# Two low-rank products side by side: decay and rate products of both directions paired on TensorE in a bidirectional recurrence

## The chip, the cores and the metric

The kernel runs on one core of one Trainium2 chip. The metric is the time of one execution on the device in microseconds (us), the median of the runs shown. PE is TensorE (its weight loads are listed apart as PEld), DVE VectorE, ACT ScalarE, POOL GpSimd and SP SyncE.

## What is computed

The program is one inference step of a two-layer backbone over 384 tokens: 128 context tokens and 256 latent tokens, with the same weights. Each layer is a SwiGLU feed-forward block, three token mixers from one input projection (grouped attention, differential attention, a bidirectional RWKV-7 recurrence), their gated merge, and a second feed-forward block. The change is inside the recurrence. Cut to what matters there:

```
w_logit = w0[d] + tanh(wl[:, d]) @ w2[d]           # decay, a low-rank product (rank 64) for each direction d
decay   = exp(-exp(-softplus(-w_logit) - 0.5))
a       = sigmoid(a0[d] + al[:, d] @ a2[d])        # rate, a low-rank product (rank 64) for each direction d
# for each head and direction, over time:
sa = S @ (-kk_t)
S  = S * w_t + outer(sa, kk_t * a_t) + outer(v_t, k_t)
o_t = S @ r_t
```

The product before the decay is 384 tokens by rank 64 by 512 channels, for two directions; the one before the rate is of the same size.

## The kernel before

The 512 channels of the recurrence are worked in four blocks (j = 0 to 3, NB = 4) of 128 channels, two heads of 64 each. In each layer one loop over j holds everything. The 384 tokens are cut into NQ = 6 chunks of 64. In block j the kernel builds the chunk products (`gram`, six parts p = 0 to 5, three of each direction), inverts the triangular systems of all chunks in five doubling levels (`level_lx`, `level_xlx`), and turns keys for later use (`turn_tok`). Between these pieces it runs the scan over chunks of the block before, s = j - 1 (`scan_right`, `scan_solve`, `scan_update`, four steps each, i = 0 to 3), and prepares decay, rate and norm of the block after, j + 1 (`prepare_decay`, `prepare_rate`, `prepare_norm`). Block 0 has no scan beside it, block 3 has no preparation in it, and the scan of block 3 runs alone behind the loop.

The order on each engine is the order in which the code is written, and engines meet only through semaphores. The same loop is written out once for PE, once for ACT, once for DVE and once for POOL. For one direction d of the block to come, PE makes the decay product (`prepare_decay`, L1221), ACT takes its tanh out of the bank into `sg` (L1723), POOL scales it (L2012), and DVE sums it over time (L2400) and centres the sums (L2405 to L2412). The rate product (L1229) goes through a tanh of ACT into `aa` (L1732), and then, behind the second level, through `key_factor` on ACT, POOL and DVE.

The quarter-size matmuls of the recurrence are issued by `quads` (L1166): one on partitions 0 to 63 and one on partitions 64 to 127. Each float32 matmul of the program stands in the trace as two MATMUL instructions. The two low-rank weights of decay lie in `lora_w`, direction 0 on partitions 0 to 63 and direction 1 on partitions 64 to 127, and so do their inputs, and the same holds for `lora_a`; so a decay or rate product reads 64 partitions and writes all 128 of a bank of 384 columns.

The eight banks of PSUM are `acc[0..3]` and `pb[0..3]`. In blocks 1 to 3 both directions of the decay share `acc[3]`, one after the other, so that PE waits for ACT's read between them. The rates use `acc[1]` (direction 0) and `acc[0]` (direction 1). `gram` part p uses `pb[(p + 2) % 4]`. For block 0 the two decay products stand one behind the other, into `pb[2]` and `pb[3]`, ahead of the loop, and so do its two rate products.

## Time and profile before

| | us |
|---|---|
| median of three runs (lowest, highest) | 2705.01 (2704.34, 2706.89) |
| the profiled execution, its own time | 2699.4 |
| its span, from first to last instruction | 2695.2 |
| loop over the blocks, layer 1 | 753.3 to 951.5 |
| scan of the last block, layer 1 | 951.5 to 967.5 |
| start of the loop, layer 2 | 2078.1 |

PE is busy for 94% of the span, DVE for 52%, ACT for 39%, POOL for 12%; the mean granted clock of TensorE is 0.965 of full speed. A busy share is an average over all stages. Times within the span are read from the timeline; a matmul's end is modelled, so distances on PE are best taken from start to start.

### The profile page before, as it was taken

Reading aid. Unit: us, or ns where it says so; the run is one execution under the profiler, and the core shown is the slowest. Engines: PE = TensorE matmul, PEld = TensorE weight load, DVE = VectorE, ACT = ScalarE, POOL = GpSimd, SP = SyncE. Lnnn points to the kernel's source line nnn. Section 1 sums busy time; section 2 is a strip of 40 time slices with the busy share of each in tenths; the row PEclk is TensorE's granted clock in tenths of the full one; section 3 lists DMA queues with packets and bytes.
Section 4 is the critical chain, followed back from the end, with each engine's and each line's share of the span. In section 5 each row is a group of like instructions: output and inputs, shape, how many; then the busy total and the mean of one; then the engine's idle time right before and its main releaser. Section 6 shows DMA issues by size and latency. Waiting matters only on the chain. (4 is left out here: it accounts for less than half of the span.)

```text
span 2695.2 us, 56725 instructions
## 1 busy us (share of the span) xinstructions
PE 2524.0 (94%) x23398; PEld 2350.4 (87%) x23398; DVE 1389.2 (52%) x2314; ACT 1056.5 (39%) x1705; POOL 332.1 (12%) x316
## 2 busy tenths in 40 slices
PE   5999999999979989999979999999998999899998
PEld 3889989889968878999968899998897888889997
DVE  3334365576576645443353334656765775544434
ACT  3333244355533424332253333434564342343323
POOL 0000032000033304000100001210001341130001
PEclk7999999999989988999989999999998999889998
DMA  8766634233200013446466665333221001234373
GB/s 270 244 219 194 189 96 125 85 89 87 88 2 4 27 45 93 126 126 202 121 211 220 225 189 156 98 108 96 83 84 62 4 4 30 80 100 127 116 218 106
DMA packets 482186, 319.95 MB, mean 119 GB/s; under 512 B 15474, under 2 KB 438920, under 8 KB 481800
## 3 DMA queue, kind: packets, MB, share of 16 engines
q1 hardware_dynamic: 481928, 316.32, 38.7%
q8 instruction: 186, 3.05, 0.5%
q14 instruction: 72, 0.59, 0.1%
HBM read 311.30 MB, written 4.98 MB: 117 GB/s over the span
## 5 line engine op out<-in xcount | busy, mean ns | idle before, releaser
L826 PE MATMUL acc<-xm_hi,w_hi 128*128 128x384 f32 x2512 | 866.8, 345 | 54.1 <-DVE xm_lo L2086 33.1
L828 PE MATMUL acc<-xm_hi,w_lo 128*128 128x384 f32 x2512 | 850.0, 338 | 0.0
L827 PE MATMUL acc<-xm_lo,w_hi 128*128 128x384 f32 x2448 | 826.7, 338 | 0.0
L2076 DVE TENSOR_TENSOR w_lo<-raw,w_hi 128x1024 fp32r<-128x1024 f32 (+1 forms) x420 | 519.7, 1237 | 503.7 <-ACT w_hi L1524 495.4
L826 PEld LDWEIGHTS acc<-xm_hi,w_hi 128*128 128x128 f32 x2512 | 479.3, 191 | 97.4 <-issue 59.0
L1524 ACT ACTIVATE w_hi<-raw 128x1024 fp32r<-128x1024 f32 (+1 forms) x420 | 439.6, 1047 | 301.6 <-PE acc L828 220.2
L828 PEld LDWEIGHTS acc<-xm_hi,w_lo 128*128 128x128 f32 x2512 | 478.8, 191 | 0.0
L827 PEld LDWEIGHTS acc<-xm_lo,w_hi 128*128 128x128 f32 x2448 | 466.6, 191 | 0.5
L826 PE MATMUL acc<-h_hi,w_hi 128*128 128x384 f32 x704 | 242.5, 345 | 8.6 <-DVE w_lo L2076 8.6
L827 PE MATMUL acc<-h_lo,w_hi 128*128 128x384 f32 x704 | 239.7, 341 | 0.0
L828 PE MATMUL acc<-h_hi,w_lo 128*128 128x384 f32 x704 | 239.7, 340 | 0.0
L1555 ACT ACTIVATE sa<-acc 128x384 f32<-128x384 f32 x88 | 43.3, 492 | 448.4 <-PE acc L828 448.2
L826 PEld LDWEIGHTS acc<-h_hi,w_hi 128*128 128x128 f32 x704 | 133.8, 190 | 19.8 <-issue 18.6
L827 PEld LDWEIGHTS acc<-h_lo,w_hi 128*128 128x128 f32 x704 | 134.0, 190 | 0.0
L828 PEld LDWEIGHTS acc<-h_hi,w_lo 128*128 128x128 f32 x704 | 133.7, 190 | 0.0
L2163 DVE TENSOR_TENSOR hf<-sa,acc 128x384 f32<-128x384 f32 x88 | 48.8, 554 | 160.6 <-PE acc L828 155.4
L1962 POOL TENSOR_TENSOR ln_sum<-x 128x384 f32<-128x384 f32 x12 | 17.2, 1431 | 920.7 <-DVE x L2099 920.5
L2008 POOL TENSOR_TENSOR ltm<-lt,cst 128x384 f32<-128x384 f32 x80 | 87.4, 1092 | 169.4 <-PE pb L1166 97.0
L2099 DVE SCALAR_TENSOR_TENSOR x<-acc,modv,x 128x128 f32<-128x128 f32 x96 | 35.7, 413 | 127.8 <-PE acc L828 127.4
L2012 POOL TENSOR_SCALAR sg<-sg 128x384 f32<-128x384 f32 x16 | 9.1, 568 | 609.8 <-ACT sg L1723 609.6
L1782 ACT ACTIVATE tl<-pb 128x384 f32<-128x384 f32 x80 | 39.3, 492 | 102.8 <-PE pb L1166 102.7
L1166 PE MATMUL pb<-xi,ltm 64*64 64x64 f32 x1920 | 71.5, 220 | 5.6 <-DVE xt L2471 2.8
(340 smaller groups left out, 3268.1 us busy)
## 6 DMA issues: line engine op xcount, KB each, us to landing
raw<-in_ffn_w_in SPq DMA_DIRECT2D x179, 512.0 KB, 4.0
modw<-in_w_mod SPq DMA_DIRECT2D x71, 1024.0 KB, 6.2
raw<-in_w_in SPq DMA_DIRECT2D x114, 512.0 KB, 4.1
raw<-in_ffn_w_out SPq DMA_DIRECT2D x64, 512.0 KB, 4.9
raw<-in_ffn_w_out SPq DMA_DIRECT2D x32, 384.0 KB, 3.5
raw<-in_w_up SPq DMA_DIRECT2D x24, 512.0 KB, 3.5
modx<-in_w_mod SPq DMA_DIRECT2D x9, 1024.0 KB, 12.8
raw<-in_w_out SPq DMA_DIRECT2D x16, 512.0 KB, 4.1
```

Source lines behind the costliest of these rows:

```text
L826: pe.matmul(out, lhs[0], rhs[0], start=first, stop=False)
L827: pe.matmul(out, lhs[0], rhs[1], start=False, stop=False)
L828: return pe.matmul(out, lhs[1], rhs[0], start=False, stop=last)
L1166: mm = pe.matmul(out[hp], lhs[hp], rhs[hp], start=start, stop=stop, skip_group_check=True)
L1524: done(act.activation(w_hi[:, c % SPL, 0:w], raw[:, c % RAW, 0:w], ACT.Copy), hi_done)
L1555: freed(act.activation(sa[:, j % 2, :], gbank(ka)[:, 0:TOK], ACT.Silu), ka)
L1782: done(act.activation(tl[:, NQ * d:NQ * d + NQ, :].rearrange("p q s -> p (q s)"), pb[d][:, 0:TOK], ACT.Copy), tl_ready)
L1962: add = lambda out, a, b: pool.tensor_tensor(out, a, b, ALU.add)
L2008: done(pool.tensor_tensor(ltm[:, u, :], lt[:, u, :], over(cst[:, o:o + CH], NQ), ALU.mult), ltm_ready)
L2076: done(dve.tensor_tensor(w_lo[:, c % SPL, 0:w], raw[:, c % RAW, 0:w], w_hi[:, c % SPL, 0:w].bitcast(F32), ALU.subtract), lo_done)
L2099: ins = dve.scalar_tensor_tensor(out=x[:, m, a:b], in0=gbank(key)[:, a:b], scalar=modv[:, 3 * s + 2, m, gi:gi + 1], in1=x[:, m, a:b], op0= ...
L2163: freed(dve.tensor_tensor(hf[:, j % 2, :], sa[:, j % 2, :], gbank(kb)[:, 0:TOK], ALU.mult), kb)
```

## The change

The decay product of direction 1 moves up, to stand right behind that of direction 0, and gets a bank of its own, `pb[1]`. The rate product of direction 0 moves down, to stand right ahead of that of direction 1; their banks, `acc[1]` and `acc[0]`, stay. ACT's tanh of the rate of direction 0 moves with it; ACT's two decay tanhs keep their places and read the new bank. Waits follow: the second decay product no longer waits for ACT's read of the first, but for the last reader of `pb[1]` in the block before (`xt_ready`, for block 0 `kk_ready`); `gram` part 3, which is next to write `pb[1]`, waits for both tanhs (`decay_done`), and `turn_tok`, the next to write `acc[3]`, for the first only. No instruction is added or taken out.

```diff
@@ -1213,9 +1213,11 @@
                         if j == 0:
                             bank = pb[2 + d]
                         else:
-                            bank = acc[3]
-                            if d == 1:
-                                pe.wait_ge(decay_done, 2 * j + 1)
+                            bank = (acc[3], pb[1])[d]
+                            if d == 1 and j == 1:
+                                pe.wait_ge(kk_ready, 1)
+                            elif d == 1:
+                                pe.wait_ge(xt_ready, 2 * (NL + 1) * (j - 1))
                             elif j >= 3:
                                 pe.wait_ge(out_done, j - 2)
@@ -1236,8 +1238,10 @@
                             pe.wait_ge(ab_ready, 2 * j + d + 1)
                         if p >= 4:
                             pe.wait_ge(gram_read, n - 3)
+                        elif p == 3 and j + 1 < NB:
+                            pe.wait_ge(decay_done, 2 * j + 4)
                         elif j == 0:
-                            pe.wait_ge((rate_done, rate_done, kk_std, kk_ready)[p], (1, 2, 1, 1)[p])
+                            pe.wait_ge((rate_done, rate_done, kk_std)[p], (1, 2, 1)[p])
@@ -1256,7 +1260,7 @@
                         if k >= 1:
                             pe.wait_ge(tok_ready, 4 * j + k)
                         elif j + 1 < NB:
-                            pe.wait_ge(decay_done, 2 * j + 4)
+                            pe.wait_ge(decay_done, 2 * j + 3)
@@ -1412,11 +1416,10 @@
                         if nxt:
                             prepare_decay(j + 1, 0)
+                            prepare_decay(j + 1, 1)
                         gram(j, 1)
                         if old:
                             scan_solve(s, 0)
-                        if nxt:
-                            prepare_decay(j + 1, 1)
                         gram(j, 2)
@@ -1443,8 +1446,6 @@
                         if old:
                             scan_right(s, 3)
-                        if nxt:
-                            prepare_rate(j + 1, 0)
                         level_lx(j, 1, 1)
@@ -1454,6 +1455,7 @@
                             scan_update(s, 3)
                         if nxt:
+                            prepare_rate(j + 1, 0)
                             prepare_rate(j + 1, 1)
                         level_xlx(j, 1, 1)
@@ -1719,7 +1721,7 @@
-                        bank = acc[3] if j >= 1 else pb[2 + d]
+                        bank = (acc[3], pb[1])[d] if j >= 1 else pb[2 + d]
@@ -1860,8 +1862,6 @@
                         if old:
                             scan_right(s, 3)
-                        if nxt:
-                            prepare_rate(g0)
                         level_lx(j, 1, 1)
                         copy_tok(j, 1, 1)
@@ -1870,6 +1870,7 @@
                         if old:
                             copy_new(s)
                         if nxt:
+                            prepare_rate(g0)
                             prepare_rate(g1)
```

The decay pair on PE, in block 1. Line numbers of the kernel before and of the changed one differ by two from there on. Before, from the end of the first `scan_right` on (`lora_w` is the decay product, `ar,bt` and `ar,kt` are `gram` parts, `rs,xt` is `scan_solve`):

```order
L1166 MATMUL acc<-ar,sp 64x64 x4
L1221 MATMUL acc<-cmix,lora_w 128x384
L1166 MATMUL pb<-ar,bt 64x128 [waits xi_ready]
L1166 MATMUL pb<-ar,bt 64x128
L1166 MATMUL pb<-ar,kt 64x128 x2
L1166 MATMUL pb<-ar,bt 64x128 x2
L1166 MATMUL pb<-ar,kt 64x128 x2
L1166 MATMUL acc<-rs,xt 64x64 [waits xt_ready,r_ready]
L1166 MATMUL acc<-rs,xt 64x64 x7
L1221 MATMUL acc<-cmix,lora_w 128x384 [waits decay_done]
L1166 MATMUL pb<-ar,bt 64x128 [waits xt_ready]
L1166 MATMUL pb<-ar,bt 64x128
```

After:

```order
L1166 MATMUL acc<-ar,sp 64x64 x4
L1223 MATMUL acc<-cmix,lora_w 128x384
L1223 MATMUL pb<-cmix,lora_w 128x384 [waits xt_ready]
L1166 MATMUL pb<-ar,bt 64x128 [waits xi_ready]
L1166 MATMUL pb<-ar,bt 64x128
L1166 MATMUL pb<-ar,kt 64x128 x2
L1166 MATMUL pb<-ar,bt 64x128 x2
L1166 MATMUL pb<-ar,kt 64x128 x2
L1166 MATMUL acc<-rs,xt 64x64 [waits xt_ready,r_ready]
L1166 MATMUL acc<-rs,xt 64x64 x7
L1166 MATMUL pb<-ar,bt 64x128 [waits xt_ready]
L1166 MATMUL pb<-ar,bt 64x128
```

The second decay product now stands ahead of `gram` part 1 and of `scan_solve`, in `pb`.

The rate pair on PE, in block 0. Before (`xi,ltm` is `level_lx`, `cst,kt` is `turn_tok`, `tl,xt` and `xt,tl` are `level_xlx`, `lora_a` is the rate product):

```order
L1166 MATMUL pb<-xi,ltm 64x64 [waits xi_ready,ltm_ready]
L1166 MATMUL pb<-xi,ltm 64x64 x11
L1229 MATMUL acc<-cmix,lora_a 128x384
L1166 MATMUL pb<-xi,ltm 64x64 [waits xi_ready,ltm_ready]
L1166 MATMUL pb<-xi,ltm 64x64 x11
L1166 MATMUL acc<-cst,kt 64x64 [waits tok_ready]
L1166 MATMUL acc<-cst,kt 64x64 x11
L1166 MATMUL pb<-tl,xt 64x64 [waits gram_read,xt_ready,tl_ready]
L1166 MATMUL pb<-tl,xt 64x64 x11
L1166 MATMUL pb<-xt,tl 64x64 x12
L1229 MATMUL acc<-cmix,lora_a 128x384
```

After:

```order
L1166 MATMUL pb<-xi,ltm 64x64 [waits xi_ready,ltm_ready]
L1166 MATMUL pb<-xi,ltm 64x64 x11
L1166 MATMUL pb<-xi,ltm 64x64 [waits xi_ready,ltm_ready]
L1166 MATMUL pb<-xi,ltm 64x64 x11
L1166 MATMUL acc<-cst,kt 64x64 [waits tok_ready]
L1166 MATMUL acc<-cst,kt 64x64 x11
L1166 MATMUL pb<-tl,xt 64x64 [waits gram_read,xt_ready,tl_ready]
L1166 MATMUL pb<-tl,xt 64x64 x11
L1166 MATMUL pb<-xt,tl 64x64 x12
L1231 MATMUL acc<-cmix,lora_a 128x384 x2
L1166 MATMUL pb<-tl,xt 64x64 [waits gram_read,xt_ready,tl_ready]
```

The first rate product has left its place between the two halves of `level_lx` and stands beside the second.

ACT's side of the rates, in block 1. Before (`tl` is the copy behind `level_lx`, `aa` the tanh of a rate, `cs` and `sg` exponentials of the decay, `osum` the copy of the scan's output):

```order
L1782 ACTIVATE tl<-pb 128x384 [waits tl_done,tok_ready]
L1788 ACTIVATE rs<-acc 128x128 [waits r_done,tl_ready]
L1732 ACTIVATE aa<-acc,half_bias 128x384 [waits ab_ready,lora_rate,r_ready]
L1782 ACTIVATE tl<-pb 128x384 [waits tl_done,rate_done]
L1777 ACTIVATE ktok<-acc 128x384 [waits tok_t,tl_ready]
L1752 ACTIVATE cs<-zi 128x384 [waits z_ready,tok_ready]
L1757 ACTIVATE sg<-sg 128x384 [waits act_chain]
L1799 ACTIVATE sld<-acc 128x2x64 [waits spo_t,act_chain]
L1732 ACTIVATE aa<-acc,half_bias 128x384 [waits ab_ready,lora_rate,snew_ready]
L1795 ACTIVATE osum<-acc 128x384 [waits o_done,rate_done]
L1782 ACTIVATE tl<-pb 128x384 [waits tl_done,o_read]
L1782 ACTIVATE tl<-pb 128x384 [waits tl_done,tl_ready]
```

After:

```order
L1784 ACTIVATE tl<-pb 128x384 [waits tl_done,tok_ready]
L1790 ACTIVATE rs<-acc 128x128 [waits r_done,tl_ready]
L1784 ACTIVATE tl<-pb 128x384 [waits tl_done,r_ready]
L1779 ACTIVATE ktok<-acc 128x384 [waits tok_t,tl_ready]
L1754 ACTIVATE cs<-zi 128x384 [waits z_ready,tok_ready]
L1759 ACTIVATE sg<-sg 128x384 [waits act_chain]
L1801 ACTIVATE sld<-acc 128x2x64 [waits spo_t,act_chain]
L1734 ACTIVATE aa<-acc,half_bias 128x384 [waits ab_ready,lora_rate,snew_ready]
L1734 ACTIVATE aa<-acc,half_bias 128x384 [waits ab_ready,lora_rate,rate_done]
L1797 ACTIVATE osum<-acc 128x384 [waits o_done,rate_done]
L1784 ACTIVATE tl<-pb 128x384 [waits tl_done,o_read]
L1784 ACTIVATE tl<-pb 128x384 [waits tl_done,tl_ready]
```

The tanh of direction 0 now comes behind the exponentials and the copy of the state, right ahead of that of direction 1 and of the copy of `osum`.

## Rows read from the trace of the kernel before

**Rows 1.** The page of the profile: head, and the engines of the chain that ended last.

```profile
span 2695.2 us, 56725 instructions
...
PE 42%; DVE 4%; ACT 1%; SPq 1%; issue 1%; DMA 0%; POOL 0%; DVEq 0%; ACTq 0%; POOLq 0%
```

**Rows 2.** Busy time by stretch: length, PE, PEld, DVE, ACT, POOL, PEclk, DMA share, GB/s.

```profile
753.20:764.20 11.00, 10.90 (x92) 7.99 (x92) 5.49 (x9) 2.49 (x6) 2.72 (x4) 0.54 0.01 1
...
796.79:849.10 52.31, 50.73 (x1335) 45.58 (x1334) 35.82 (x66) 22.02 (x45) 17.06 (x18) 1.00 0.01 4
```

**Rows 3.** Timeline of PE ahead of block 0: start, duration, what, [idle before].

```profile
734.95 0.92 PE L1221 MATMUL pb<-cmix,lora_w 64*128 64x384 f32 x4
735.79 0.44 PE L826 MATMUL acc<-br_hi,w_hi 128*128 128x384 f32 x1
```

**Rows 4.** Timeline of PE, block 1 (801 to 805) and block 2 (863 to 865).

```profile
801.85 0.63 PE L1166 MATMUL acc<-rs,xt 64*64 64x64 f32 x16
802.41 0.91 PE L1221 MATMUL acc<-cmix,lora_w 64*128 64x384 f32 x2
803.25 0.43 PE L1166 MATMUL pb<-ar,bt 64*64 64x128 f32 x4
803.52 0.39 PE L1166 MATMUL pb<-ar,kt 64*64 64x128 f32 x4
...
804.17 0.63 PE L1166 MATMUL acc<-sas,btok 64*64 64x64 f32 x16
...
863.50 0.63 PE L1166 MATMUL acc<-rs,xt 64*64 64x64 f32 x16
863.97 0.39 PE L1166 MATMUL pb<-ar,bt 64*64 64x128 f32 x4
864.19 0.39 PE L1166 MATMUL pb<-ar,kt 64*64 64x128 f32 x4
```

**Rows 5.** Timeline of DVE, blocks 0 and 1, and the last recurrence.

```profile
771.02 0.56 DVE L2458 TENSOR_TENSOR xi<-pb,cst 128x384 f32<-128x384 f32 x1
...
803.09 0.42 DVE L2492 COPY sas<-acc 128x256 f32<-128x256 f32 x1
...
816.64 0.29 DVE L2492 COPY sas<-acc 128x128 f32<-128x128 f32 x1 [0.28 <-PE acc L1166]
...
955.43 0.42 DVE L2492 COPY sas<-acc 128x256 f32<-128x256 f32 x1 [1.89 <-PE acc L1166]
```

**Rows 6.** Timeline of PE, last recurrence of layer 1.

```profile
955.91 0.68 PE L1166 MATMUL acc<-sas,btok 64*64 64x64 f32 x16 [0.59 <-DVE sas L2492]
```

**Rows 7.** Timeline of PE, start of block 0 of layer 1.

```profile
758.67 1.64 PE L1221 MATMUL acc<-cmix,lora_w 64*128 64x384 f32 x2
760.24 0.69 PE L1166 MATMUL pb<-ar,bt 64*64 64x128 f32 x4
...
762.00 1.44 PE L1166 MATMUL acc<-cst,bt 64*64 64x64 f32 x24
763.28 0.38 PE L1166 MATMUL pb<-ar,bt 64*64 64x128 f32 x4
```

**Rows 8.** Timeline of PE around rate products, blocks 0 and 1.

```profile
771.28 0.91 PE L1229 MATMUL acc<-cmix,lora_a 64*128 64x384 f32 x2
772.12 0.92 PE L1166 MATMUL pb<-xi,ltm 64*64 64x64 f32 x24
...
819.88 0.45 PE L1166 MATMUL acc<-sp,ar 64*64 64x64 f32 x8 [1.06 <-DVE sp L2475]
...
820.73 0.91 PE L1229 MATMUL acc<-cmix,lora_a 64*128 64x384 f32 x2
821.57 0.91 PE L1166 MATMUL pb<-xi,ltm 64*64 64x64 f32 x24
```

**Rows 9.** Timeline of ACT behind the second rate product, block 1.

```profile
826.82 0.49 ACT L1795 ACTIVATE osum<-acc 128x384 f32<-128x384 f32 x1
828.48 0.49 ACT L1782 ACTIVATE tl<-pb 128x384 f32<-128x384 f32 x1 [1.16 <-PE pb L1166]
```

## The prediction

> **What bounds the kernel now.** I read the page first, then the busy times by stretch, then the timelines of PE, DVE, ACT and POOL through the recurrence. The span is 2695.2 us, and in the chain that ended last PE has 42% of the span against 4% for DVE; no DMA share is seen in it [rows 1]. For this change only the loop over the blocks counts, so the next view is the busy time by stretch. In block 1 PE is busy for 50.73 of 52.31 us, at a granted clock of 1.00, with a DMA share of 0.01 [rows 2]. DVE has 35.82 us there, ACT 22.02, POOL 17.06. So PE sets the pace nearly all the time, and what is taken off PE comes off the time, as long as DVE and ACT, which must answer it, do not come too late at some place. Those places have to be looked for one by one in the timelines. The reader is to see there where PE's next instruction starts, and where the result it needs is ready.
>
> **What one low-rank product costs, and what a pair costs.** A product alone, of direction 1 in block 1, starts at 802.41 and the next instruction at 803.25: 0.84 us [rows 4]. Ahead of block 0 the trace holds the very pair that the change makes: four MATMULs, both directions, into two banks. They start at 734.95 and what follows starts at 735.79: again 0.84 us [rows 3]. Two products behind each other cost what one costs, since they read different halves of the partitions. So in each pair one product is free.
>
> The change saves a little more than 0.84, since each product also has borders with the quarter-size matmuls around it. From the start of a solve (L1166, 16 MATMULs) to the second group of `gram` matmuls it is 801.85 to 803.52, 1.67 us, with a product between; without one, in block 2, the same two pieces take 863.50 to 864.19, 0.69 us [rows 4]. The difference is 0.98 us: that is what PE itself saves when a product leaves its place. The page "TensorEngine Tiling (Array Packing)" of the Trainium skill, section Key Properties, says that a change of tiling mode drains TensorE. The 0.14 us by which 0.98 exceeds 0.84 agrees with it; by the page's "up to 2x" of the section Theoretical Speedup alone one would count 0.84 for a pair, 10.1 us for twelve.
>
> There are three preparations in a layer (blocks 0, 1 and 2), two kinds, two layers: 12 pairs. I follow each to the next place where PE waits.
>
> **Decays in blocks 1 and 2.** The pair takes the place of the first product, so `gram` part 1 and `scan_solve` start when they did. Behind the solve `gram` part 2 starts 0.98 earlier, and so could `scan_update`, now at 804.17 [rows 4], at 803.19. But it needs the solved states that DVE copies (L2492): that copy runs from 803.09 to 803.51 [rows 5], and it does not get earlier, because what it waits for (`gram` part 1 and the solve) stands ahead of the removed product. From the end of such a copy to PE's start it is 0.06 us: 955.43 + 0.42 = 955.85, and 955.91 [rows 5, 6]. So the update starts at 803.57 and the gain here is 0.60 instead of 0.98; PE gets a new wait of 0.38 behind this copy. Block 2 repeats the pattern. Four times 0.60 is 2.4 us.
>
> Does the 0.60 last? Behind this point DVE is at times the late one: PE waits 1.06 us at 819.88 for the new state [rows 8]. But DVE's run of work that ends in that state starts with the copy at 816.64, which itself waited for PE [rows 5]. So the wait moves forward with PE and stays 1.06.
>
> The added waits: the second decay product asks for the last level of the block before, which DVE wrote before PE came to the first product; `gram` part 3 asks for both tanhs of ACT, and two pieces of PE work stand between. I cost both at nothing. Late, each would hold all of PE behind it, one for one; I keep up to 0.3 us each for four places, 1.2 us, as the bad bound.
>
> **Decays in block 0.** There is no scan beside it, and nothing behind the removed product waits for its neighbours. But TensorE has just stood still, waiting for DVE, and runs at the low level: the granted clock is 0.54 over the first 11 us, which is 1.2 GHz for nearly all of it and 2.4 GHz only from about 763 on [rows 2]. The product takes 1.57 us there, 758.67 to 760.24; a later piece that starts at 762.00 takes 1.28, and from 763.28 on all is short [rows 7]. If the rise comes at the same moment of the stage as before, the slow stretch is as long as before, and what moves into it in place of the product would have been run at the full clock later: then the gain is that of the full clock, 0.98, say 1.0. If the rise came after the same amount of work instead, the gain would be 1.57 and borders, about 1.7. I take 1.0, since the rows show the clock rising in the middle of a piece of work and at no border of it. Twice, 2.0 us, with 3.4 as the upper end. Further on in block 0 PE waits for DVE, but that run of DVE's work starts from ACT's copy of `gram` part 3, which moves with PE.
>
> **Rates in blocks 1 and 2.** The product at 820.73 goes, and `level_lx` of direction 1 starts in its place [rows 8]. What it reads has been ready: its `xi` is written right before the state for which PE waited at 819.88 [rows 8]. Behind it come a turn of keys, the solve, and the first half of a level, whose inputs from ACT are copies that move up too. So the whole 0.98 stays, four times: 3.9 us.
>
> What the moved tanh can do on ACT: at its new place ACT has two tanhs, then the copy of `osum`, which ended at 827.31, then the copy behind level 2, which started at 828.48 after 1.16 us of waiting for PE [rows 9]. One tanh more, about 0.6 us (two of these copies' 0.49 or a little more), fits into 1.16. So I cost it at nothing; without that cover, up to 0.1 us per block.
>
> **Rates in block 0.** Here the cover is thinner. `level_lx` of direction 1 starts at 772.12 behind the product at 771.28 [rows 8]; it could start 0.98 earlier, but its `xi` is written by DVE from 771.02 to 771.58 [rows 5], and 0.06 later is 771.64. Its gain is 0.48. DVE's run of work ahead of it moves with PE. Twice, 1.0 us.
>
> **The sum.** 2.4 + 2.0 + 3.9 + 1.0 = 9.3 us, from 12 pairs that would give 11.8 at 0.98 each if nothing were late. The stages behind the recurrence start from its last output through DVE, ACT and POOL, so they move as a whole, and their weights are asked for as PE frees buffers. Against the profiled execution (span 2695.2, own time 2699.4) that is 2685.9 and 2690.1. The median of the runs shown is 5.6 above that execution's own time, and I keep this distance: 2705.0 - 9.3 = 2695.7 us.
>
> **The rivals.**
> A, the forecast, 2695.7; its own range is 2693.0 to 2698.5. Chance 0.68.
> B, nothing is late and the slow stretch gives back fully: 8 x 0.98 + 2 x 0.98 + 2 x 1.7 = 13.2 us, 2691.8. For it: DVE has 16 us of free time in a block. Against it: the two copies of [rows 5] stand at fixed places. Chance 0.08.
> C, a shift is lost on the way. If the DVE or ACT runs do not move with PE (their backlog starts earlier than I read), the decays' 2.4 and half of the rest go: about 5 us remain, 2700. For it: the 1.06 us wait shows that DVE is late at one place in each of these blocks. Against it: DVE waited for PE at 816.64 [rows 5]. Chance 0.14.
> D, the change does not do what it says: `acc[3]` with `pb[1]`, or the wait between the two products, keeps them apart, and a pair takes 2 x 0.84. Then a product is only moved. The rates give nothing; the decay pair delays `gram` part 1, the solve and DVE's copy by 0.84, the update is then late by about 0.4 in four places, and the time is 2705 + 1.6 = 2706.6. Against it: the pair of [rows 3], and the same for rates ahead of block 0. Chance 0.05.
> E, slower: the clock. In block 0 PE's first 10 us run at 1.2 GHz; with two products side by side its work there has another mix. If the slow stretch lasted twice as long, work of 5 us at the full clock would cost 10, 5 us more per layer, and 10 us in all would outweigh the 9.3: 2705.7; it decides from about 9 us of further slow time in each layer. Later stages rise from 1.2 GHz too, and each could come out a microsecond or two away from before, to either side; that together with this could bring 2708. Against it: a removed product leaves no gap, PE goes on without a pause (10.90 of 11.00 us busy, [rows 2]). The page "TensorE: Matmul & The Clock Gate" of the Trainium skill, in its Part 1, says that the clock follows how busy the engine has been; no row here shows that a pair counts as less busy. Chance 0.05.
>
> **How the numbers follow.** Range: A and the part of C and B next to it, 2691.5 to 2700.5, leaves out half of B, D, E and the far part of C, about 0.18. About 0.2% (5.4 us) is what a measurement of this kernel tells from no change. Faster by more than that: A, B and a third of C, 0.81. Within it: the rest of C, D and part of E, 0.16. Slower: 0.03.
>
> **What would show it.** In the changed kernel's timeline of PE: groups of four MATMULs of 64x384 that last 0.84 from start to start (1.57 in block 0's decays), six per layer in the loop; a wait of about 0.4 for DVE's copy L2492 (two lines further on) ahead of the first `scan_update` in blocks 1 and 2; a short wait ahead of the second `level_lx` of block 0; the 1.06 wait for the state unchanged. Block 1 should last 52.31 - 1.6 = 50.7 us from first `gram` to first `gram`, block 2 1.6 less, block 0 1.5 less, block 3 the same. The prediction is wrong if block 3 or the stages behind change, if a pair lasts 1.6 at the full clock, or if the wait for the state grows by what was saved before it.

## The result, and the profile after

The changed kernel takes 2689.51 us (median of four runs, 2685.39 to 2691.22); the kernel before, run beside it, takes 2704.68 (2703.26 to 2706.89). The ratio over the single runs is 0.9941, with a 95% interval of 0.9926 to 0.9957, so the change is a gain of about 0.6%: 15.2 us in this first comparison, where 9.3 were predicted. The time lies below the predicted range of 2691.5 to 2700.5. More runs of both, further down, make the difference 13.2.

Page of the changed kernel, the lines that answer to [rows 1], and the busy time of the engines:

```profile
span 2686.4 us, 56725 instructions
...
PE 2513.9 (94%) x23398; PEld 2347.4 (87%) x23398; DVE 1392.8 (52%) x2314; ACT 1054.1 (39%) x1705; POOL 328.4 (12%) x316
...
PE 42%; DVE 4%; ACT 1%; SPq 1%; issue 1%; DMA 0%; POOL 0%; DVEq 0%; ACTq 0%; POOLq 0%
```

The number of instructions and the shape of the chain have not changed. The next view is the busy time by stretch, as in [rows 2]: the first 11 us of block 0 in layer 1, then the same in layer 2.

```profile
754.40:765.40 11.00, 10.05 (x172) 8.56 (x174) 8.28 (x14) 3.53 (x9) 2.71 (x4) 0.85 0.01 1
...
2076.00:2087.00 11.00, 10.46 (x153) 8.86 (x155) 7.08 (x12) 3.04 (x8) 2.63 (x4) 0.72 0.01 1
```

PE does 172 instructions there in place of 92, at a granted clock of 0.85 in place of 0.54. No instruction was taken out, so this is the first sign that the gain is not only that of products side by side: PE also comes to the full clock earlier. The timeline of PE shows where the clock rises, in layer 1:

```profile
754.49 0.69 PE L1166 MATMUL pb<-ar,bt 64*64 64x128 f32 x4 [12.18 <-DVE kt L2437]
...
756.39 1.00 PE L1223 MATMUL acc<-cmix,lora_w 64*128 64x384 f32 x1
756.40 1.00 PE L1223 MATMUL pb<-cmix,lora_w 64*128 64x384 f32 x1
...
757.86 0.44 PE L1166 MATMUL pb<-ar,bt 64*64 64x128 f32 x4
758.13 0.39 PE L1166 MATMUL pb<-ar,kt 64*64 64x128 f32 x4
...
769.68 0.92 PE L1166 MATMUL pb<-xi,ltm 64*64 64x64 f32 x24 [0.37 <-DVE xi L2459]
```

The first `gram` group lasts 0.69, which is the low level (1.2 GHz); right behind the decay pair, 3.37 us after the block's start, the same group lasts 0.44, which is the high one (2.4 GHz). Before, `gram` groups were still long at 760.24, 6.9 us after the start, and short only at 763.28, 10.0 us after it [rows 7]. In layer 2 the rise comes 6.08 us after the start, at 2082.10. The last row is the short wait for `xi` ahead of the second `level_lx`.

Block 1 at full clock, where the steps of the prediction can be read singly:

```profile
797.47 0.59 PE L1223 MATMUL acc<-cmix,lora_w 64*128 64x384 f32 x1
797.48 0.59 PE L1223 MATMUL pb<-cmix,lora_w 64*128 64x384 f32 x1
...
798.32 0.44 PE L1166 MATMUL pb<-ar,bt 64*64 64x128 f32 x4
...
800.36 0.39 PE L1166 MATMUL pb<-ar,kt 64*64 64x128 f32 x4
800.96 0.68 PE L1166 MATMUL acc<-sas,btok 64*64 64x64 f32 x16 [0.22 <-DVE sas L2493]
...
816.74 0.45 PE L1166 MATMUL acc<-sp,ar 64*64 64x64 f32 x8 [1.08 <-DVE sp L2476]
...
821.08 0.92 PE L1231 MATMUL acc<-cmix,lora_a 64*128 64x384 f32 x4
821.93 0.92 PE L1166 MATMUL pb<-tl,xt 64*64 64x64 f32 x24
```

And DVE at the place that bounds the update:

```profile
800.48 0.42 DVE L2493 COPY sas<-acc 128x256 f32<-128x256 f32 x1
```

Both products of a direction pair start within 0.01 us of each other, and what follows starts 0.85 after the first (797.47 to 798.32, and again 821.08 to 821.93). The copy ends at 800.90 and the update starts at 800.96.

The lengths of the blocks carry the rest. In this table a block goes from its first `gram` to the first `gram` of the next, and "rise" is the time from the start of block 0 to the first group of matmuls that is short. The whole recurrence goes from the start of block 0 to the start of the last group of matmuls in the last scan.

| layer 1 / layer 2, us | rise | block 0 | block 1 | block 2 | block 3 | whole recurrence |
|---|---|---|---|---|---|---|
| before (second profile) | 9.8 / 9.8 | 43.49 / 43.49 | 52.88 / 52.88 | 53.32 / 53.31 | 48.35 / 48.36 | 213.54 / 213.52 |
| after (second profile) | 3.4 / 6.1 | 39.87 / 40.89 | 51.36 / 51.36 | 51.79 / 51.81 | 48.37 / 48.37 | 206.87 / 207.91 |

The recurrence (the four blocks and the last scan) gives 6.67 + 5.61 = 12.3 us. Block 3 and the last scan (15.5 us) are as before.

### The profile page after: what moved, and what is told of

It is laid out like the page before. It is cut to its first block and busy times, and to the rows that moved or that the text cites. A ratio compares the mean times of both kernels' runs of the same rounds, so it can differ in the third digit from the quotient of the medians.

```text
span 2686.4 us, 56725 instructions
## 1 busy us (share of the span) xinstructions
PE 2513.9 (94%) x23398; PEld 2347.4 (87%) x23398; DVE 1392.8 (52%) x2314; ACT 1054.1 (39%) x1705; POOL 328.4 (12%) x316
```

## The experiments

Times are medians, each with the kernel before beside it on the same chip; n is the number of runs. The ratio, with its 95% interval in brackets, is formed over the single runs and can differ a little from that of the two medians. Lengths of blocks and rises come from the one profiled execution of each kernel. Spare products read the same inputs as real ones. The result of every spare product or matmul is overwritten unread, so the outputs do not change.

**1. Both kernels again, unedited.**

> The kernel before, unchanged, profiled and timed again, to see how much one profiled execution differs from the next. Theory 1 (the paired product makes TensorE's clock rise earlier in block 0): block 0 of both layers again lasts about 43.5 us from first gram to first gram, with the granted clock rising some 9 to 10 us after its start, and the time is 2704 to 2705. Theory 2 (the moment of the rise varies from execution to execution, whatever the kernel): block 0's slow stretch differs from the 9 to 10 us seen by a few us in at least one layer, and single executions scatter by several us.

> The changed kernel, unchanged, profiled and timed again. Theory 1: block 0 again rises to the full clock 3 to 6 us after its start and lasts about 40 to 41 us, against 43.5; the median is about 2690, 14 to 15 us below the kernel before. Theory 2: the slow stretch of block 0 falls anywhere between 3 and 10 us; over more executions the gain settles nearer to 9 to 10 us (2695), which is what the pairs save at the full clock.

Before again: 2703.41 (n 11) against 2702.70 (n 23), ratio 0.9999 [0.999, 1.0008], so the comparison itself is even. After again: 2689.48 (n 5) against 2702.70, 0.9946 [0.9932, 0.9959], 13.2 us. The spans of these two profiles, 2699.5 and 2686.7, differ by 12.8, of which the table gives 12.3 to the recurrence. Single executions scatter: those of the kernel before lie between 2697.34 and 2704.55 here. The profile on which the prediction's sum rests (span 2695.2) was one 4.3 us below this one, with the same lengths inside the recurrence to 0.2 us; it spent less time at the low clock elsewhere (mean granted clock 0.965 against 0.960). So the comparison of four runs with four holds scatter, and the recurrence is what the change moves.

**2. The change without its decay pair in block 0.** From the changed kernel; in block 0 the second product keeps its old place and bank (the waits of `gram` part 3 and `turn_tok` and ACT's bank follow, not shown).

```diff
-                            bank = (acc[3], pb[1])[d]
+                            bank = (acc[3], pb[1] if j >= 2 else acc[3])[d]
                             if d == 1 and j == 1:
-                                pe.wait_ge(kk_ready, 1)
+                                pe.wait_ge(decay_done, 3)
...
-                            prepare_decay(j + 1, 1)
+                            if old:
+                                prepare_decay(j + 1, 1)
                         gram(j, 1)
                         if old:
                             scan_solve(s, 0)
+                        else:
+                            prepare_decay(j + 1, 1)
```

> The change, but in block 0 the two decay products stay apart as before (into one bank). Theory 1: block 0 goes back to a slow stretch of 9 to 10 us and the time rises by 2 x 3 = 5 to 6 us over the changed kernel, to about 2695. Theory 2: only the product's own saving of about 1 us per layer is lost, 2 us over the changed kernel, and the slow stretch scatters as in the others.

2694.18 (n 7) against 2702.70, 0.9972 [0.9961, 0.9983]; span 2689.1. Timeline of PE in block 0:

```profile
757.01 1.64 PE L1223 MATMUL acc<-cmix,lora_w 64*128 64x384 f32 x2
...
760.48 1.64 PE L1223 MATMUL acc<-cmix,lora_w 64*128 64x384 f32 x2
...
763.82 1.13 PE L1166 MATMUL acc<-cst,bt 64*64 64x64 f32 x24
764.78 0.38 PE L1166 MATMUL pb<-ar,bt 64*64 64x128 f32 x4
```

The rise is back at 9.7 / 9.8 us and block 0 at 43.12 / 43.10, while blocks 1 and 2 keep their gain. The pair in block 0 alone is thus worth 43.12 - 39.86 = 3.26 and 43.10 - 40.86 = 2.24, together 5.5 us, where I had put 2.0. What is left in block 0, 43.49 - 43.11, is the rate pair's 0.38.

**3. Only the pair of block 0.** From the kernel before (ACT's bank follows).

```diff
-                            bank = acc[3]
-                            if d == 1:
+                            bank = pb[1] if j == 1 and d == 1 else acc[3]
+                            if d == 1 and j == 1:
+                                pe.wait_ge(kk_ready, 1)
+                            elif d == 1:
...
                             prepare_decay(j + 1, 0)
+                            if j == 0:
+                                prepare_decay(j + 1, 1)
...
-                        if nxt:
+                        if nxt and old:
                             prepare_decay(j + 1, 1)
```

> The kernel before with the decay pair in block 0 alone. Theory 1: gains 2.2 to 3.2 us per layer, about 5.5 us in all, 2699, with the clock rising 3 to 6 us after the start of block 0. Theory 2: gains about 1 us per layer, 2 us in all, 2703.

2697.94 (n 11) against 2702.70, 0.9981 [0.9972, 0.999]: 4.8 us. Block 0 lasts 40.26 / 41.27, the rise is at 3.4 / 6.1, and blocks 1 and 2 are as before. In the recurrence that is 3.2 + 2.2 = 5.4 us.

**4. Only the rate pairs.** From the kernel before, both `prepare_rate` as in the change (ACT's too).

```diff
-                        if nxt:
-                            prepare_rate(j + 1, 0)
                         level_lx(j, 1, 1)
...
                         if nxt:
+                            prepare_rate(j + 1, 0)
                             prepare_rate(j + 1, 1)
```

> The kernel before with the rate pairs alone, decays as before. By the prediction's steps block 0 is shorter by 0.4 to 0.5 us and blocks 1 and 2 by 0.98 us each: 43.1, 51.9 and 52.3 us. A rival, that the moved tanh on ACT or the later rate costs something further on: less than that, with a wait of PE for ACT behind the second level.

This kernel was executed once, in 2691.55 us. Single executions scatter too much for that to tell a gain; the lengths of the blocks do tell. Blocks 1 and 2 last 51.89 and 52.34, so 0.99 and 0.98 less than before, in both layers; block 0 lasts 43.11 / 43.12, 0.38 less. Rates in all: 4 x 0.98 + 2 x 0.38 = 4.7 us (predicted 4.9). What the decays add in the full change is then 51.89 - 51.36 = 0.53 in block 1 and 52.34 - 51.80 = 0.54 in block 2.

**5. Is it the saved work, or what stands beside it?** Two kernels from the one before, with a spare product in block 0 behind the first: on the other half of the partitions, so that it runs beside the real one, or on the same half, so that it runs behind it. Nothing is saved in either.

```diff
                             prepare_decay(j + 1, 0)
+                            if j == 0:
+                                pe.wait_ge(kk_ready, 1)
+                                pe.matmul(pb[1][:, 0:TOK], lora_w[HALVES[1], 128:256], cmix[HALVES[1], 12, :], start=True, stop=True)
```

(`HALVES[0]` in both places for the product behind.)

> The kernel before, with one spare decay product of direction 1 (its result is overwritten unread) issued right behind the first decay product of block 0 into the free bank pb[1]; both real products stay where they were. Theory 1a (two products side by side bring the clock's rise forward): nothing is saved in work, yet block 0 rises to the full clock 3.4 us (layer 1) and 6.1 us (layer 2) after its start, and lasts about 41.2 and 42.2 us against 43.5, 3 to 4 us less in all. Theory 1b (it is the missing second product, so a change of what follows, that matters): the rise stays at 9.8 us and block 0 at 43.5.

> The same, but the spare product reads the same half of the partitions as the first one (direction 0 again), so that the two can't run side by side and take 3.1 us at the low clock instead of 1.6. Theory 1a: no two halves are at work at once, so the rise stays at 9 to 10 us after the start, and block 0 is 0.8 to 1.6 us longer than 43.5. A third reading (any more work early on brings the rise forward): the rise comes early here too.

Timeline of PE with the spare product beside:

```profile
756.43 1.00 PE L1221 MATMUL acc<-cmix,lora_w 64*128 64x384 f32 x1
756.44 1.00 PE L1417 MATMUL pb<-cmix,lora_w 64*128 64x384 f32 x1
...
757.89 0.44 PE L1166 MATMUL pb<-ar,bt 64*64 64x128 f32 x4
...
758.91 0.91 PE L1221 MATMUL acc<-cmix,lora_w 64*128 64x384 f32 x2
```

The same in layer 2, where all of the pair runs at the low clock:

```profile
2077.90 1.00 PE L1221 MATMUL acc<-cmix,lora_w 64*128 64x384 f32 x1
2077.91 1.00 PE L1417 MATMUL pb<-cmix,lora_w 64*128 64x384 f32 x1
...
2079.48 0.69 PE L1166 MATMUL pb<-ar,bt 64*64 64x128 f32 x4
```

And with the spare product behind, in layer 1:

```profile
756.90 1.64 PE L1221 MATMUL acc<-cmix,lora_w 64*128 64x384 f32 x2
758.34 1.48 PE L1417 MATMUL pb<-cmix,lora_w 64*128 64x384 f32 x2
```

Beside, block 0 falls from 43.49 to 40.89 / 42.21 with the rise at 3.4 / 6.5, although all the old work and one product more are still there. In layer 2 the second real product, which stands alone, starts 5.4 us after the block's start and is running when the clock rises. Behind, block 0 grows to 45.59 / 45.36 with the rise at 13.8 / 13.6. The pair takes 2077.90 to 2079.48, 1.58 us, as long as the lone product of the kernel before (1.57 us, [rows 7]) and in its place, so it is not the length of the lone product that holds the rise back, but the missing neighbour.

The run with the spare product beside also splits the 3.23 and 2.22 us that block 0 won in experiment 3: 2.60 and 1.28 come from the clock alone, and 40.89 - 40.26 = 0.63 and 42.21 - 41.27 = 0.94 from the product that is gone. The medians are 2702.21 (n 10), 0.9997 [0.9988, 1.0006], and 2707.47 (n 10), 1.0013 [1.0004, 1.0022], against 2703.60. The second agrees with its blocks (about +4). The first gains less than its two recurrences do (210.93 + 212.61 against 427.06, 3.5 us): its profiled execution was the fastest of the ten, and whether the rise comes as early in the other nine stays open. By the medians alone, this kernel is not told from the kernel before.

**6. Does it take a pair at all?** Three orders of block 0's start. First, from the changed kernel, the pair behind `gram` part 1 and the solve:

```diff
-                            prepare_decay(j + 1, 0)
-                            prepare_decay(j + 1, 1)
                         gram(j, 1)
                         if old:
                             scan_solve(s, 0)
+                        if nxt:
+                            prepare_decay(j + 1, 0)
+                            prepare_decay(j + 1, 1)
```

(ACT takes the two tanhs behind its `gram` copy as well.)

> The changed kernel with the decay pair moved behind gram part 1 and scan_solve (on PE) and both tanhs behind the copy of gram part 1 (on ACT). If the step on DVE's copy was right (that copy bounded the gain to 0.6 in blocks 1 and 2, because its inputs stood ahead of the product), the wait of 0.22 ahead of the first scan_update goes, and blocks 1 and 2 are about 0.4 us shorter each, and block 2 by up to 0.4 more since the product no longer waits for osum; 1.6 to 2.4 us in all. If the copy was not the bound, blocks 1 and 2 stay at 51.4 and 51.8. In block 0 the pair comes about 1.9 us later, which by theory 1a may put off the clock's rise by one to three us.

```profile
757.07 0.45 PE L1166 MATMUL pb<-ar,kt 64*64 64x128 f32 x4
757.45 0.59 PE L1223 MATMUL acc<-cmix,lora_w 64*128 64x384 f32 x1
...
849.88 0.68 PE L1166 MATMUL acc<-rs,xt 64*64 64x64 f32 x16 [0.89 <-ACT rs L1790]
```

The clock rises at 3.0 / 6.1, in layer 1 before the pair comes: `gram` parts 0 and 1 on end are enough. 2689.07 (n 5) against 2703.60, 0.9942 [0.9928, 0.9955], which the scatter does not tell from the changed kernel's time. Block 1 is 0.43 shorter than in the changed kernel, since DVE's copy is now hidden behind the pair. Block 2 gains nothing and is 0.17 longer, as the last row shows: the solve stands too early for ACT's copy `rs` and waits 0.89. So the 1.6 to 2.4 us that were expected did not come.

Second, therefore, the pair between `gram` part 1 and the solve:

```diff
                         gram(j, 1)
+                        if nxt:
+                            prepare_decay(j + 1, 0)
+                            prepare_decay(j + 1, 1)
                         if old:
                             scan_solve(s, 0)
```

> The changed kernel with the decay pair between gram part 1 and scan_solve (on PE), both tanhs behind the copy of gram part 1 (on ACT). In the run before, the pair behind the solve took away the wait for DVE's copy but gave block 2 a wait of 0.9 us for ACT's copy ahead of the solve. Here the pair covers that one as well, and gram part 2 (0.87 us) covers the way from the solve over DVE's copy to the update (0.28 + 0.42 + 0.06 = 0.76 us). If the waits are what bounds: block 1 about 50.9 us, block 2 about 50.95 us (against 51.36 and 51.8), 1.2 us less per layer, block 0 as in the run before (40.0 and 40.9), the median about 2 us below the changed kernel. If something else bounds them, blocks 1 and 2 stay above 51.3.

Both waits are gone, and so is one of 0.4 us for DVE's `osum` ahead of block 2's first product, which both kernels of the comparison have: block 1 lasts 50.93, block 2 51.07, against 51.36 and 51.80 of the changed kernel. The recurrence is 205.63 / 206.74. Timed, 2690.10 (n 5) against 2703.23, 0.9956 [0.9942, 0.9969]: the 2.4 us by which its recurrence beats the changed kernel's do not stand out of the scatter, and the median about 2 us below the changed kernel's did not show.

Third, from the kernel before, no pair anywhere: in block 0 PE does `gram` part 0, part 1, then a lone product, part 2, the other lone product (ACT in the same order).

```diff
-                        if nxt:
+                        if nxt and old:
                             prepare_decay(j + 1, 0)
...
                         if nxt:
-                            prepare_decay(j + 1, 1)
+                            prepare_decay(j + 1, int(old))
                         gram(j, 2)
+                        if not old:
+                            prepare_decay(1, 1)
```

> The kernel before, with block 0's two decay products moved later and kept apart: gram parts 0 and 1, product, gram part 2, product, turn_tok. No pair anywhere in the loop. Theory 1a (side by side work brings the rise forward) expects the rise at 9 to 10 us after the start, as in the kernel before, and block 0 at 43.5. Theory 1b' (it is a lone product, which keeps only half of the rows at work for 1.6 us at the low clock, that holds the rise back, and gram parts alone do not) expects layer 1 to rise at about 3.0 us, as when gram parts 0 and 1 followed each other, and block 0 of layer 1 at about 40.9 (two lone products at the full clock); layer 2 rose later than layer 1 in every kernel with a pair, and may rise at 6 or at 9 us.

```profile
756.25 0.69 PE L1166 MATMUL pb<-ar,bt 64*64 64x128 f32 x4 [12.18 <-DVE kt L2440]
...
759.26 0.67 PE L1166 MATMUL pb<-ar,kt 64*64 64x128 f32 x4
759.86 0.91 PE L1221 MATMUL acc<-cmix,lora_w 64*128 64x384 f32 x2
...
763.35 0.92 PE L1166 MATMUL acc<-cst,bt 64*64 64x64 f32 x24 [0.72 <-ACT sg L1725]
```

The rise is at 3.6 in layer 1 and under 3 in layer 2 (6 or 9 were expected there), the first lone product is already short, and block 0 lasts 41.16 / 40.81, in spite of a new wait of 0.72 for ACT. 2694.92 (n 6) against 2703.23, 0.9969 [0.9957, 0.9981]. So the pair is not what brings the rise forward. What is common to all early cases is that no product stands alone in the first 5 us of the slow stretch.

**7. The counter-test.** From `pair_before_solve`'s order, with its pair, one lone spare product ahead of `gram` part 1.

```diff
+                        if j == 0:
+                            pe.matmul(acc[3][:, 0:TOK], lora_w[HALVES[0], 128:256], cmix[HALVES[0], 12, :], start=True, stop=True)
                         gram(j, 1)
```

> The version with the pair between gram part 1 and the solve, in which block 0 rose to the full clock at 2.6 to 3.0 us (layer 1) and 6.1 us (layer 2), plus one spare lone decay product of direction 0 in block 0 between gram part 0 and gram part 1 (overwritten unread). Theory 1b' (a lone product early in the stretch holds the rise back): the rise goes back to 9 to 10 us in both layers and block 0 to about 43 to 44 us, though the pair is still there behind gram part 1. Theory 1a (a pair brings it forward, or any early work does): the rise stays at or below 6 to 7 us and block 0 at 41.5 to 42.5 us, longer only by the spare product's own 1.6 us at the low clock.

```profile
758.07 1.64 PE L1418 MATMUL acc<-cmix,lora_w 64*128 64x384 f32 x2
...
761.55 1.00 PE L1223 MATMUL acc<-cmix,lora_w 64*128 64x384 f32 x1
...
763.12 0.69 PE L1166 MATMUL pb<-ar,bt 64*64 64x128 f32 x4
...
764.88 1.22 PE L1166 MATMUL acc<-cst,bt 64*64 64x64 f32 x24
765.94 0.38 PE L1166 MATMUL pb<-ar,bt 64*64 64x128 f32 x4
```

One product alone puts the rise back to 9.8 / 9.8, with the pair in place, and block 0 to 43.11 / 43.09: 3.31 and 2.17 us more than without it, for 1.6 us of work. 2692.61 (n 9) against 2703.40, 0.9954 [0.9941, 0.9968]; the medians of the two kernels, 10.8 and 13.1 us below the kernel before, differ in the same direction.

**8. No slow stretch.** Block 0 starts slow because PE has waited 12.2 us for DVE. From the changed kernel, that wait is filled with 15 spare matmuls on all 128 partitions; then the same 15, and 18, in the order of `pair_before_solve`.

```diff
+                pe.wait_ge(kk_std, 1)
+                for _ in range(15):
+                    pe.matmul(pb[0][:, 0:TOK], blk, cmix[:, 12, :], start=True, stop=True)
```

> The changed kernel with 15 spare full-size matmuls (overwritten unread) in PE's wait of 12.2 us ahead of block 0. If the slow stretch comes from PE standing still there, block 0 runs at the full clock from its start, and is shorter by half of the slow 3.4 and 6.1 us: about 1.6 and 2.9 us, 4.5 us in all, 2685. If not, it stays at 39.9 and 40.9 us.

> The same with the 15 spare matmuls in the wait ahead of block 0, the best version that the runs point to. Blocks 38.3, 50.9, 50.95, 48.4 and 15.5 us in both layers, 204.1 against 206.9 and 207.9 of the changed kernel, 6.5 us less in all; median about 2683 to 2685.

> The version with the pair between gram part 1 and the solve and 18 instead of 15 spare full-size matmuls in the wait ahead of block 0: the 15 took 9.94 us and left 2.3 us of standing still, in which the clock fell in one layer of one execution and not in the other three. 18 take 11.9 us of the 12.2. Expected: block 0 at the full clock from its start in both layers, 38.3 to 38.5 us, the whole recurrence 204.2 us per layer, median 2683 to 2685. If the fall has nothing to do with the gap, one of the layers starts slow again.

With 15, `spare_in_wait` runs block 0 at full clock from its start, 38.35 / 38.36 us; 2686.97 (n 5) against 2703.60, 0.9945 [0.9931, 0.9959]. The same 15 in `pair_before_solve_warm` do it in layer 2 only (38.49); in layer 1, busy time by stretch from the last spare on:

```profile
751.00:754.36 3.36, 1.01 (x5) 0.29 (x3) 3.26 (x4) 0.00 (x0) 3.11 (x4) 0.97 0.00 0
754.36:758.00 3.64, 3.64 (x34) 3.47 (x36) 3.36 (x6) 0.33 (x2) 0.56 (x1) 0.56 0.02 5
```

The 15 leave 2.35 us of waiting, and behind it the clock is 0.56 (the last column but two); block 0 takes 40.02. The other three waits of 2.3 us, in the other layer and in `spare_in_wait`, were followed by the full clock. 2687.00 (n 5) against 2703.23, 0.9942 [0.9928, 0.9955]. With 18 the wait left is 0.39:

```profile
742.41 11.88 PE L1411 MATMUL pb<-cmix,cst 128*128 128x384 f32 x36
754.68 0.44 PE L1166 MATMUL pb<-ar,bt 64*64 64x128 f32 x4 [0.39 <-DVE kt L2439]
```

Both layers start at full clock (38.49 / 38.48). The recurrence is 205.41 / 204.32 (block 3 of layer 1 has a 0.8 us gap for which the profile shows no releaser), and the kernel takes 2684.17 us (n 6, 2678.42 to 2685.20) against 2703.40, ratio 0.9925 [0.9909, 0.994]. It has the lowest median of this study: 19.2 us below the kernel before beside it, where the changed kernel was 13.2 below its own. Of the 6.0 between them the recurrences account for 206.87 + 207.91 - 205.41 - 204.32 = 5.1. The intervals of the two ratios still touch (0.9909 to 0.994 and 0.9932 to 0.9959), so the lengths of the blocks, more than the medians, show that it is faster.

## Why the prediction was right, and where it failed

**A pair costs what one product costs.** Right: 0.85 for 0.84. Rival D, where a pair would take twice as long, is out.

**Decays in blocks 1 and 2.** Predicted 0.60 each, bounded by DVE's copy; measured 0.53 and 0.54 in each layer, 2.1 us in all for 2.4. The update itself starts 7.21 us after block 1's start before (second profile) and 6.61 after, so the 0.60 is there; the last 0.06 goes right behind the wait, where the update's own group takes 0.52 to the next start in place of 0.46. The new wait ahead of the update is there (listed as 0.22, since ends of matmuls are modelled; the groups before step by 0.22, so my estimate of the end of the last is 800.58, and of the wait 0.38). Experiment 6 shows the mechanism from the other side: with the pair behind `gram` part 1, so that it covers the copy, block 1 wins 0.43 more.

**Rates in blocks 1 and 2.** Predicted 0.98 each, measured 0.98 to 0.99. **Rates in block 0.** Predicted 0.48, measured 0.38. The wait for `xi` is there, 0.37; DVE ends it at 769.53 and PE starts at 769.68, 0.15 behind it, where I had taken 0.06:

```profile
768.97 0.56 DVE L2459 TENSOR_TENSOR xi<-pb,cst 128x384 f32<-128x384 f32 x1
```

**What was costed at nothing.** Right. The wait for the state stays at 1.08 (1.06 before), so rival C, a shift lost on the way, is out. ACT's moved tanh fits, as its timeline shows, with 0.56 of the 1.16 of waiting [rows 9] left:

```profile
822.08 1.19 ACT L1734 ACTIVATE aa<-acc,half_bias 128x384 f32<-128x384 f32 x2 [0.78 <-PE acc L1231]
823.30 0.49 ACT L1797 ACTIVATE osum<-acc 128x384 f32<-128x384 f32 x1
824.35 0.49 ACT L1784 ACTIVATE tl<-pb 128x384 f32<-128x384 f32 x1 [0.56 <-PE pb L1166]
```

**Decays in block 0: the step that failed.** "If the rise comes at the same moment of the stage as before, the slow stretch is as long as before [...] I take 1.0, since the rows show the clock rising in the middle of a piece of work and at no border of it." Predicted 2.0 us for the two layers, with 3.4 as the upper end; measured 5.5. Here the prediction failed: this term was mis-sized, and with it the time fell out of the range. The inference was the fault: that the rise falls within a piece of work says that it follows no border of the program, not that it stays at its moment when the work before it changes. It moved from 9.8 us after the block's start to 3.4 and 6.1. Both ends I had (same moment, or same amount of work) kept the slow stretch as long as before or shortened it by one product only. The ends should have reached to a block 0 with no slow stretch, and in the other direction to a longer one, as experiment 5 then produced. Rival E named the clock as what could break the forecast, but only as a loss; I gave no chance to the same mechanism with a gain. Rival B forecast 13.2 us, which is the difference of the larger set of runs, but that is luck: it had no wait behind DVE's copies, which the trace shows, and at most 1.7 us per layer for block 0's decays, where 3.3 and 2.2 were measured.

What the experiments show of the cause: a product that stands alone early in the slow stretch holds the rise back. Leaving out the pair but keeping the lone product away gives the early rise (`lone_products_later`, and `pair_after_solve` in layer 1, before its pair has come); adding one lone product takes it away with the pair present (`lone_spare_added`); and giving the lone product a neighbour, with all else as before, brings it (`spare_beside`). So the change gained in block 0 because neither of its two products stood alone any more. Of its 5.5 us about 3.9 (2.60 + 1.28, experiment 5) are clock, and 1.6 the product that is gone.

A rival to this is that the clock rises at moments of its own, and that the start of block 0 only falls differently against them. The granted clock of each stretch shows where it fell ahead of block 0, here for the changed kernel, 0.50 for the low level and 1.00 for the high one, in layer 1 and then in layer 2:

```profile
740.50:747.40 6.90, 1.80 (x10) 0.94 (x8) 5.55 (x9) 3.46 (x6) 0.90 (x2) 1.00 0.00 0
747.50:754.40 6.90, 0.00 (x0) 0.00 (x0) 6.55 (x11) 2.57 (x7) 4.56 (x5) 0.50 0.00 0
...
2062.00:2068.40 6.40, 1.83 (x10) 0.97 (x8) 5.04 (x9) 2.96 (x5) 0.94 (x2) 1.00 0.00 0
2068.50:2076.00 7.50, 0.00 (x0) 0.01 (x1) 7.12 (x12) 3.06 (x8) 4.63 (x5) 0.50 0.00 0
```

The clock fell 7.0 us ahead of block 0 in layer 1 and 7.6 us ahead in layer 2. Read in the same way, the fall in layer 2 lies 7.5 to 7.6 us ahead of block 0 in the kernel before (both profiles) and in `apart_in_block0`, `lone_spare_added`, `pair_before_solve`, `pair_block0_only`, `spare_beside` and `spare_behind` too. There the rise comes about 6 us after the start in the kernels where no product stands alone early, 9.8 with one or two that do, and 13.6 with three. So the rival does not explain the difference between these kernels.

It does bear on the difference between the layers. Where no product stands alone early, the rise came about 3 us after the start when the fall lay 7.0 to 7.5 or 10.1 to 10.4 us ahead of it, and about 6 us after when it lay 7.55 to 7.60 us ahead; in `pair_before_solve` 7.48 and 7.55 us ahead went with rises 3.3 us apart. No run moved this distance alone, so this is a pattern in the traces and not shown as a cause. If it is one, a small shift of what stands ahead of block 0 can turn the gain of 3.3 us into one of 2.2, or the other way round.

**The sum.** The recurrence gives 12.3 us for 9.3: block 0's decays +3.5, the smaller terms -0.5. What the medians show beyond 12.3 (13.2 with more runs, 15.2 at first) is no step of the sum: single executions of one kernel lie 6 to 13 us apart, and the profile of the kernel before that the sum started from was a short one. "Block 1 should last 52.31 - 1.6" began from a stretch that ended 0.75 us before block 2's first `gram`; the lengths of the second profiles are 52.88 and 51.36, and the difference, 1.5, was nearly right.

**Open:** whether the place of the fall ahead of block 0 decides between the 3.4 of layer 1 and the 6.1 of layer 2; and what in a lone product delays the rise. It is not its length (experiment 5), but it reads only half of the partitions and is also only half as many matmuls in the same time, and no run parts the two. Each kernel other than the two compared has one profiled execution. The differences of its medians from the kernel before depart from those of its recurrences by 2.1 us less in `spare_beside` (1.4 for 3.5) and 3.5 us more in `lone_products_later` (8.3 for 4.8), so the rises in the other executions are not known.

## What to carry to other kernels

Where an engine comes out of a wait into a slow stretch, read what it does there, since an edit in it can be worth more or less than its own time. Here it paid to put products that read only half of the partitions side by side, or behind the rise. Cost such an edit between no slow stretch at all and one that is half as long again. Where a bank is free, try filling the wait with spare matmuls until shortly before it ends: that is in the version with the lowest median here. And before a gain is costed on one side of a semaphore, look where the engine that answers gets its input: moving the pair by one piece of code, to between `gram` part 1 and the solve, hid DVE's copy (and in block 2 a wait for `osum` too) and was worth 0.43 us in block 1 and 0.73 in block 2.

## What the runs showed of the hardware

- The time from the end of a 12.2 us wait to the high clock, with PE busy throughout, was 2.6 to 13.8 us, by what PE ran: 13.6 to 13.8 with three products standing alone (two of them on end), 9.7 to 10.0 with two, or with one and a pair behind it, 2.6 to 6.5 with none early on. The page "TensorE: Matmul & The Clock Gate" of the Trainium skill says in Part 1 that the warm-up is an amount of time and not a number of matmuls. Here it was no fixed time either: it changed with which matmuls ran, and between two layers with the same instructions.
- A wait of 12.2 us brought the clock down in every profile, one of 2.3 us in one of four, one of 0.4 us in none of two.
- Each decay product at the low clock takes 1.57 us, and a pair 1.58 us, but a lone one added there to `pair_before_solve` cost 3.3 and 2.2 us.
- Executions of the kernel before scatter by 6 to 13 us in 2700 within a comparison, while its recurrence is the same to 0.2 us in two profiles, so that lengths of single blocks settled what medians of few runs could not.
